# Expert results kept as rows in DRAM by indirect DMA, and the loop over expert passes written out

## The reference, cut to what matters

```python
top_v, top_i = lax.top_k(logits, TOP_K)          # 2 of 8 experts per token
gates = jax.nn.softmax(top_v, axis=-1)
comb = jnp.sum(jax.nn.one_hot(top_i, N_EXPERTS) * gates[..., None], axis=1)
for e in range(N_EXPERTS):
    y = y + comb[:, e:e + 1] * ((silu(h @ we_gate[e]) * (h @ we_up[e])) @ we_down[e])
x = x + y                                        # then a final RMSNorm
```

## Time and profile before

| | |
|---|---|
| median of 3 runs | 1300.16 us (1299.64 to 1300.19) |
| the profiled execution's own time | 1300.49 us |
| its span in the profile | 1298.7 us |
| PE busy | 1247.0 us, 96% |
| DVE busy | 1033.6 us, 80% |
| ACT busy | 828.6 us, 64% |
| POOL busy | 70.6 us, 5% |
| DMA | 351.69 MB, mean 271 GB/s |
| expert passes in the span | about 502 to 1286 us |

### The profile page before, as it was taken

The page is one execution under the profiler, slowest core; times in us unless marked ns, Lnnn a source line. Parts: engine busy times, 40 slices in busy tenths (PEclk is TensorE's granted clock), DMA queues, the critical chain, the costliest instruction groups (busy, mean ns, idle before and its releaser), DMA issues.

```text
span 1298.7 us, 18756 instructions
## 1 busy us (share of the span) xinstructions
PE 1247.0 (96%) x6921; PEld 1063.0 (82%) x6921; DVE 1033.6 (80%) x963; ACT 828.6 (64%) x751; POOL 70.6 (5%) x75
## 2 busy tenths in 40 slices
PE   6988999999999988999999999999999999999996
PEld 5977899999898777888888888888888888888885
DVE  5889564444478957889989989989989989989986
ACT  5656554444455644677677677677777677677674
POOL 3220000000012000000000000000000000000000
PEclk9999999999999998999999999999999999999999
DMA  9940465566436044999999999999999999999970
GB/s 273 337 130 17 146 195 188 172 191 191 134 113 213 17 152 158 348 381 355 343 383 350 347 380 350 344 382 348 346 382 350 345 381 348 348 380 353 340 288 32
DMA packets 180166, 351.69 MB, mean 271 GB/s; under 512 B 8678, under 2 KB 68380, under 8 KB 180124
## 3 DMA queue, kind: packets, MB, share of 16 engines
q1 hardware_dynamic: 178108, 343.77, 75.7%
q0 software_dynamic: 2016, 7.34, 1.6%
HBM read 348.99 MB, written 2.10 MB: 270 GB/s over the span
## 4 chain that ended last, share of the span: by engine, by line
PE 81%; DVE 11%; ACT 2%; issue 2%; SPq 1%; DMA 1%; DVEq 0%; ACTq 0%
PE YB L1619 20%; PE WBS L1606 13%; PE WBS L1607 12%; PE WBS L1608 12%; PE YB L1324 5%; DVE acc L848 4%; PE WBS L1264 3%; PE WBS L1266 3%; PE WBS L1265 3%; DVE w_lo L787 2%; PE YB L1307 2%; PE YB L1634 1%; DVE att L890 1%; DMA raw<-in_w_in 1%; ACT w_hi L488 1%
## 5 line engine op out<-in xcount | busy, mean ns | idle before, releaser
L787 DVE TENSOR_TENSOR w_lo<-raw,w_hi 128x2048 fp32r<-128x2048 f32 x325 | 739.1, 2289 | 124.6 <-ACT w_hi L488 121.1
L488 ACT ACTIVATE w_hi<-raw 128x2048 fp32r<-128x2048 f32 x325 | 617.4, 1916 | 147.6 <-PE YB L1619 67.2
L1606 PE MATMUL WBS<-w_hi,t_hi 128*128 128x512 f32 (+1 forms) x768 | 290.5, 378 | 1.4 <-DVE t_lo L1194 1.4
L1607 PE MATMUL WBS<-w_lo,t_hi 128*128 128x512 f32 (+1 forms) x768 | 285.8, 372 | 0.0
L1608 PE MATMUL WBS<-w_hi,t_lo 128*128 128x512 f32 (+1 forms) x768 | 285.7, 372 | 0.0
L1606 PEld LDWEIGHTS WBS<-w_hi,t_hi 128*128 128x128 f32 x768 | 144.6, 188 | 26.2 <-issue 1.5
L1608 PEld LDWEIGHTS WBS<-w_hi,t_lo 128*128 128x128 f32 x768 | 144.4, 188 | 26.2
L1607 PEld LDWEIGHTS WBS<-w_lo,t_hi 128*128 128x128 f32 x768 | 144.6, 188 | 24.3
L1264 PE MATMUL WBS<-t_hi,w_lo 128*128 128x256 f32 x448 | 127.4, 284 | 0.0
L1265 PE MATMUL WBS<-t_hi,w_hi 128*128 128x256 f32 x448 | 126.7, 283 | 0.0
L1266 PE MATMUL WBS<-t_lo,w_hi 128*128 128x256 f32 x448 | 126.7, 283 | 0.0
(11 more groups left out here) (262 smaller groups left out, 1425.6 us busy)
## 6 DMA issues: line engine op xcount, KB each, us to landing
raw<-in_we_gate SPq DMA_DIRECT2D x88, 1024.0 KB, 5.4
raw<-in_we_up SPq DMA_DIRECT2D x88, 1024.0 KB, 5.6
raw<-in_we_down SPq DMA_DIRECT2D x88, 1024.0 KB, 5.9
raw<-in_w_in SPq DMA_DIRECT2D x20, 1024.0 KB, 5.7
raw<-in_wd_gate SPq DMA_DIRECT2D x11, 1024.0 KB, 5.3
raw<-in_wd_up SPq DMA_DIRECT2D x11, 1024.0 KB, 5.4
raw<-in_wd_down SPq DMA_DIRECT2D x11, 1024.0 KB, 5.0
raw<-in_w_out SPq DMA_DIRECT2D x8, 1024.0 KB, 10.9
```

What stands on the lines that cost most here:

```text
L488: act.activation(w_hi[:, hi_slot(n), :], raw[slot][:], ACT.Copy).then_inc(hi_ready, 1)
L787: dve.tensor_tensor(w_lo[slot][:], raw[slot][:], w_hi[:, hi_slot(n), :].bitcast(F32), ALU.subtract).then_inc(lo_ready, 1)
L1606: pe.matmul(bank, xs_hi[:, k0 + k, :], hi[:, k, :], start=start, stop=False)
L1607: pe.matmul(bank, xs_hi[:, k0 + k, :], lo[:, k, :], start=False, stop=False)
```

## The change

The results of the first seven experts are no longer scattered by PE. A DRAM tensor `y_rows` of 1 + 2 x 256 rows gets row 1 + t for the first choice of token t, 257 + t for its second, and row 0 for slots without a token. POOL fills it with zeros from `att` in layer 1. DVE works out the rows (`dest_of`), and a third column of `mark` carries them through `pick`. At u = 2 ACT writes the result times the gate into `h`, POOL stores it by an indirect DMA (`store_rows`), and `selT`, the low part, the scatters and their adds are gone for these seven; nor are zeros scattered in the first pass. In the eighth pass POOL loads the rows back (`load_rows`), and DVE adds them to `X` at u = 16 and u = 30 (`sum_rows`). The eighth expert's result still goes through PE at the end. The loops over passes are written out for the eight experts; a loop for further items stands behind an `If`, which isn't taken here.

```diff
         h_stored, rows_ready_at, xg_ready, xg_turned = sem("h_stored"), sem("rows_ready_at"), sem("xg_ready"), sem("xg_turned")
         rows_taken = sem("rows_taken")
 
         h_rows = nc.dram_tensor("h_rows", [T, D], F32, kind="Internal").ap()
+
+
+        y_rows = nc.dram_tensor("y_rows", [1 + 2 * T, D], F32, kind="Internal").ap()
+        STORED = NE - 1
+        SUM_AT = [16, 30]
+        zeros_stored, y_stored, y_loaded, y_summed, dest_ready = (sem(s) for s in (
+            "zeros_stored", "y_stored", "y_loaded", "y_summed", "dest_ready"))
 
         block = ctx.enter_context(nc.Block())
...
@@ -438,6 +448,10 @@
                     pool.wait_ge(added, 2 * TT)
                 pool.memset(cu[:, :, 0:PAD], 0.0).then_inc(pads_ready, 1)
                 pool.memset(att[:], 0.0).then_inc(pads_ready, 1)
+                if l:
+                    pool.wait_ge(pads_ready, 2 * L)
+                    for k in range(2 * TT):
+                        pool.dma_start(y_rows[1 + P * k:1 + P * (k + 1), :], att[:].rearrange("p r a i -> p (r a i)")).then_inc(zeros_stored, 16)
 
                 for n in range(len(LEVELS) - 1):
                     pool.wait_ge(decay_ready, 8 * l + n + 1)
...
@@ -464,13 +478,40 @@
             for t in range(TT):
                 pool.wait_ge(normed, 3 * TT + t + 1)
                 pool.dma_start(h_rows[P * t:P * (t + 1), :], h[:, t, :]).then_inc(h_stored, 16)
+            pool.wait_ge(zeros_stored, 16 * 2 * TT)
             pool.wait_ge(h_stored, 16 * TT)
             pool.wait_ge(meta_ready, 1)
-            n_items = pool.value_load(meta[0:1, 0:1], min_val=NE, max_val=ITEMS)
-            with pool.Fori(0, n_items) as i:
+            def fetch_rows(i):
+
                 pool.wait_ge(rows_ready_at, i + 1)
                 pool.sem_inc(rows_taken, 1)
                 pool.indirect_dma_start(xg[:], None, h_rows[:, :], bass.IndirectOffsetOnAxis(rows_at[:, 0:1], 0)).then_inc(xg_ready, 16)
+
+            def store_rows(i):
+
+                pool.wait_ge(y_hi_ready, i + 1)
+                pool.wait_ge(dest_ready, i + 1)
+                pool.indirect_dma_start(y_rows[:, :], bass.IndirectOffsetOnAxis(dest_at[:, i % 2:i % 2 + 1], 0), h[:, i % 2, :], None).then_inc(y_stored, 16)
+
+            def load_rows(t):
+
+                for rank in range(2):
+                    r0 = 1 + T * rank + P * t
+                    pool.dma_start(h[:, rank, :], y_rows[r0:r0 + P, :]).then_inc(y_loaded, 16)
+
+            for i in range(NE):
+                if i:
+                    store_rows(i - 1)
+                if i == STORED:
+                    pool.wait_ge(y_stored, 16 * STORED)
+                    load_rows(0)
+                fetch_rows(i)
+            pool.wait_ge(y_summed, 2)
+            load_rows(1)
+            last = pool.value_load(meta[0:1, 0:1], min_val=NE - 1, max_val=ITEMS - 1)
+            with pool.If(last > NE - 1):
+                with pool.Fori(NE - 1, last) as k:
+                    fetch_rows(k + 1)
 
 
         @block.scalar
...
@@ -540,6 +581,8 @@
                 def coarse(n):
 
                     act.wait_ge(level_done, 9 * l + n + 1)
+                    if l and n == 1:
+                        act.wait_ge(zeros_stored, 16 * 2 * TT)
                     s = LEVELS[n]
                     for r in range(2):
                         bank = YB[:, 2 * (n % 2) + r, :]
...
+
                 preload(ACT.Silu)
                 for u in range(N_FF):
                     if u >= 2:
                         hi(MOE0 + u, i)
-                    if u == 2:
+                    if u == 2 and prev is not None:
 
                         act.wait_ge(unit_used, i * N_FF + MOE0)
-                        y_part()
+                        if stored:
+                            if prev >= 2:
+                                act.wait_ge(y_stored, 16 * (prev - 1))
+                            act.activation(h[:, prev % 2, :], YB[:, 0:2, :].rearrange("p a c -> p (a c)"), ACT.Copy,
+                                           scale=slot_gate[:]).then_inc(y_hi_ready, 1)
+                        else:
+                            y_part()
                     for c in range(EC):
                         if TURN[c] + 2 == u:
                             act.wait_ge(eT_done, i * EC + (c + 1))
...
@@ -1100,6 +1158,8 @@
 
             dve.tensor_tensor(lead[:, :, 0], top[:, :, 1], top[:, :, 0], ALU.subtract).then_inc(lead_ready, 1)
             dve.tensor_tensor(chosen, first, second, ALU.add).then_inc(choice_ready, 1)
+            step(dve.tensor_scalar(score, second, float(T), 1.0, ALU.mult, ALU.add))
+            step(dve.tensor_tensor(dest_of[:].rearrange("p e t -> p t e"), score, each(mark[:, :, 0:1]), ALU.add))
             dve.wait_ge(lead_exp, 1)
             step(dve.tensor_scalar(lead[:, :, 2], lead[:, :, 1], 1.0, None, ALU.add))
             step(dve.reciprocal(lead[:, :, 3], lead[:, :, 2]))
...
-                dve.tensor_copy(picked[:], bank[:, 0:2]).then_inc(picked_ready, 1)
-
-            def turn_rows(count):
-
-                dve.wait_ge(picked_ready, count)
-                dve.tensor_scalar(selT[:], token_row[:], picked[:, 0:1], None, ALU.is_equal)
+                dve.tensor_copy(picked[:], bank[:, 0:3]).then_inc(picked_ready, 1)
+
+            def turn_rows(i, stored):
+
+                dve.wait_ge(picked_ready, i + 1)
+                if stored:
+                    if i:
+                        dve.wait_ge(y_hi_ready, i)
+                    if i >= 2:
+                        dve.wait_ge(y_stored, 16 * (i - 1))
+                    dve.tensor_copy(dest_at[:, i % 2:i % 2 + 1], picked[:, 2:3]).then_inc(dest_ready, 1)
+                else:
+                    dve.wait_ge(y_hi_ready, i)
+                    dve.tensor_scalar(selT[:], token_row[:], picked[:, 0:1], None, ALU.is_equal)
                 dve.tensor_copy(slot_gate[:], picked[:, 1:2]).then_inc(selT_ready, 1)
 
 
             for t in range(TT):
                 ins = dve.tensor_scalar(sel[:, t, :], slot_no[:], place[:, t, 0:1], None, ALU.is_equal)
             ins.then_inc(sel_ready, 1)
+            dve.tensor_copy(mark[:, :, 2], dest_of[:, 0, :])
             dve.tensor_copy(mark[:, :, 1], comb[:, :, 0]).then_inc(cur_ready, 1)
 
             step(dve.tensor_copy(slot_of[:, 0:NE, :].rearrange("p e t -> p t e"), place))
...
-            dve.wait_ge(y_zeroed, 1)
-            with dve.Fori(0, n_items) as i:
+            def sum_rows(t):
+
+                dve.wait_ge(y_loaded, 16 * 2 * (t + 1))
+                for rank in range(2):
+                    ins = dve.tensor_tensor(X[:, t, :], X[:, t, :], h[:, rank, :], ALU.add)
+                    ins.then_inc(y_summed, 1)
+                    dve.wait_ge(y_summed, 2 * t + rank + 1)
+                if t:
+                    dve.memset(started[:, 0:1], 0.0).then_inc(y_lo_ready, STORED)
+                    dve.memset(started[:, 1:2], 0.0).then_inc(scattered, 4 * STORED)
+                    dve.memset(started[:, 2:3], 0.0).then_inc(quad_added, 4 * STORED)
+
+            def expert(i, prev, stored=True):
+
                 for u in range(N_FF):
                     if u >= 2:
                         lo(MOE0 + u, i)
-                    if u == 2:
-                        y_part(i + 1)
+                    if u == 2 and not stored:
+                        y_part(i)
+                    if stored and i == STORED and u in SUM_AT:
+                        sum_rows(SUM_AT.index(u))
                     for r in range(4):
-                        if SCATTER[r] + 2 == u:
-                            add_quad(r, i * 4 + (r + 1), YB[:, 2, :])
+                        if not stored and SCATTER[r] + 2 == u:
+                            add_quad(r, prev * 4 + (r + 1), YB[:, 2, :])
                     for c in range(EC):
                         if TURN[c] + 2 == u:
                             dve.wait_ge(eT_hi_ready, i * EC + (c + 1))
...
                 for u, (what, c, part) in enumerate(plan):
@@ -1619,13 +1708,13 @@
                                     ins = pe.matmul(YB[:, half, :], a[:, f, :], w[:, k, HALF * half:HALF * (half + 1)],
                                                     start=(first and s), stop=(last and e))
                     ins.then_inc(unit_used, 1)
-                    if u in SCATTER:
+                    if u in SCATTER and not stored:
                         r = SCATTER.index(u)
                         if r == 0:
-                            pe.wait_ge(y_hi_ready, i + 1)
-                            pe.wait_ge(y_lo_ready, i + 1)
+                            pe.wait_ge(y_hi_ready, i)
+                            pe.wait_ge(y_lo_ready, i)
                         else:
-                            pe.wait_ge(quad_added, i * 4 + (r + 1))
+                            pe.wait_ge(quad_added, prev * 4 + (r + 1))
                         scatter(r, YB[:, 2, :])
                     if u in TURN:
                         tc = TURN.index(u)
...
```

(32 more changed lines are left out.)

73 lines of the change are left out of this document (39 added, 34 removed).

## The result

The changed kernel takes **1277.55 us** (median of 4 runs, 1277.48 to 1277.74), beside 1300.01 (median of 4, 1299.64 to 1300.19) for the one before: a ratio of 0.9828, interval 0.9811 to 0.9845. That is 22.5 us faster. The kernels of the experiments were timed on several chips, each beside the kernel before, whose medians there were 1300.09 to 1300.52; the ratios go by these, and microseconds of different experiments can be compared to within some 0.5.

A forecast was written before the change was run, and what follows sets the result against it. PE, full in the expert passes, was taken as the bound. The profiled 1300.49 us, less 15.7 for scatters, plus 2.7 for sums, gave 1287.5; the median, 0.33 lower, 1287.2 us; range 1284.0 to 1293.5.

The forecast's parts named there:

- The scatters: PE in the passes: dropping four scatters a pass saves 1.96 us each, 15.7 us over eight passes.
- the 0.04 over two matmuls: PE units with a scatter: slower pitch behind it; if due to the place, the gain is 14.7, not 15.7.
- DVE and ACT keep up at 2.72: Units 2 to 6 without scatters: DVE and ACT allow 2.72 us a unit, since they lose work too.
- Rival 2: DVE and ACT need 3.22 us a unit anyway, PE waits for w_lo; 1295 to 1303 us; chance 0.05.
- The sums: DVE adds in the last pass at u = 16 and 30 delay PE: 2.7 us together, between 1 and 5.3.
- Rival 4: Sums of the last pass late or dearer, loads back waiting for slow stores: 1290 to 1293 us; chance 0.08.
- Costed at nothing: Zeros, stores, loads back, DVE's router steps and loop boundary taken as free; end jump taken as 0, up to 2 us.
- the jump at the end: Each engine jumps over the unused loop after the passes: 0, up to 2 us if it loads code.
- Rival 1: Transfers become the bound at 357 GB/s, a pass needing 99.9 us: 1304 us; chance 0.06, a third reaching 1304.
- Rival 3: Written-out passes make PE load 28 more code blocks: gain gone at 0.45 us each, 1310 at 0.8; chance 0.03.
- The boundary of the loop: Between passes PE shows no gap in six of them, so writing out the loop gives nothing.
- a chain behind PE's own turns, which the change leaves alone: PE's short gaps before down units, 30 in six passes, 10.4 us in all, were expected to stay.

The follow-up runs named there:

- tiles_160: Kernel before with the unused tile idle 160 bytes larger, so later tiles stand where the changed kernel has them; 1292.95 us, ratio 0.9939.
- out_and_160: Kernel before with idle 160 bytes larger and its passes written out on all engines, scatters kept; 1290.02 us, ratio 0.9919.
- the six distances tried here: Start of eT less that of the weight parts, modulo 256 bytes, moved by resizing tiles; changed kernel 1277.55 us at 0, 1283.44 at -32.

## Why the prediction was right and where it was wrong

The 22.5 us are three things: **7.1** from the placement (1300.01 to 1292.95), **2.9** from writing out (to 1290.02), **12.5** from the exchange of scatters for stores. The prediction had the third, at 13.0 (15.7 less 2.7), and had nothing for the other two. Ends of the last unit in the four traces say much the same: 1286.2, 1278.5, 1275.4, 1263.2 us, so 7.7, 3.2 and 12.2.

These steps hold some time that need not be the code's. From the end of the mixer's last unit to the end of the passes' first the four traces take 26.9, 27.3, 26.7 and 26.3 us, at a granted clock of 0.64 to 0.67 up to the passes' first matmul, and the tail behind the last unit is 13.1 in `tiles_160` where it is 12.5 in the other three. What stands outside these two stretches (the passes, where PE ran at the full clock, and the 1.5 us before them) gives **8.0** for the placement (1.5 before the passes, 6.5 in them), **2.5** for writing out and **11.7** for the exchange, and 0.7 is left for the stretch between.

- **The scatters: right as a difference, a little too dear as a price.** u = 3 to 6 fell to 2.72, 2.72, 2.72 and 3.20, 1.95 a pass for a forecast of 1.96. But 0.14 of it was the placement of `selT`, and four scatters cost 1.81 where the tiles lie well. I had seen the 0.04 over two matmuls and had asked whether it "belongs to the place and not to the scatter", meaning the place in the order of the work. It belonged to the place in memory. The lower end, 14.7, was the better value of this term: measured 8 x 1.82 = 14.6.
- **DVE and ACT keep up at 2.72: right.** Rival 2 fell; PE shows no wait for `w_lo` from 595 to 1170 us.
- **The sums: right,** 2.77 for 2.7, in size and in place: 1.57 at unit 17 (forecast 1.5), 0.95 at unit 30 and 0.27 at unit 32 (forecast 1.2 for the two). Rival 4, dearer sums, fell too.
- **Costed at nothing, and so it was:** the stores, issued seven times from 599.0 to 1168.8 us and landed after 7.0 us in the median; the loads back, which landed in time for DVE at 1209.83 without an idle time ahead of it; the zeros, with which the last unit before the passes ends at 477.24, as it does in `out_and_160`, which has none; the jump at the end, which stands in PE's and DVE's idle time behind the last unit, 12.5 us before and after. PE waits there as it did:

```profile
1265.82 0.47 PE L1667 MATMUL WBS<-t_hi,selT 128*128 128x512 f32 x1 [2.62 <-DVE t_lo L1236]
```

- **Rival 1, the transfers, fell.** 377 GB/s at a share of 1.03 in the passes, and 393 with four times the stores, for 200 us on end. The row that had spoken against it, 400 GB/s over 8 us, was the right one; the share of 1.00 in the earlier trace rows was no limit.
- **Rival 3, code loading, fell.** The queue of code (q8) carries 57 packets, 0.93 MB, over the whole span, where it was 29; these are the 28 more that the rival had counted. They cost nothing: from 700 to 1100 us PE is busy 399.96 of 400.
- **Wrong: "The boundary of the loop: PE shows no gap in six of them, since the stretch of rows 2 is full, so writing it out gives nothing."** The boundary does cost nothing: over it the first matmul follows the last by 0.23 us, the usual pitch. But a loop's price isn't only at its boundary. It was in PE's short gaps before down units, which I took for "a chain behind PE's own turns, which the change leaves alone". At u = 8 half of the 0.5 us between the last matmul of unit 7 and the first of the down unit was PE's register steps and separate waits. The range's lower end allowed for "the shorter waits of constants helping PE's gaps a little"; measured it is 0.22 a pass for PE, 0.31 with all engines, 2.5 us over the eight passes and 2.9 by the medians.
- **Missing: a term for where the tiles lie.** "I take 15.7, since the rest of the unit is the same code" treats the same code as the same time, and the sum carries over all that lies outside the scatters unchanged, the down units at 2.81 us among it. Two new tiles and a longer one, 160 bytes in all, took 7 to 8 us off work that the change doesn't mention; a down unit then took 2.72. It could have been asked beforehand: 12 matmuls of one shape took 2.72 us in gate and up units and 2.81 in down units (the first timeline above), with nothing waited for in either. This is the main cause of the miss: 1277.55 and 7.1 are 1284.6, just inside the range. With both terms away the exchange alone would have given 1300.01 - 12.5 = 1287.5, beside the forecast of 1287.2.

The Trainium skill ("Runtime: NRT & Kernel Launch", "Instruction fetch mechanics") advises to unroll, because of stalls for fetching at taken branches. Unrolling did pay here. But what it saved stands at u = 8, behind a wait, and not at the branch back, so no run here shows that reason. The prediction said that by this rule the loop before would lose time at every pass; but the queues of code move nothing between 620 and 1200 us in the kernel before, so nothing was fetched at the branch back and the rule's case didn't arise.

## What to carry to other kernels

A change that adds or resizes any tile moves all later ones, and that alone can be worth more than the change; before a difference is put down to the code, run the old kernel with dead bytes in the place of the new tiles, and compare the pitch of matmuls that nobody touched. Where PE is full, try stationary and streamed tiles that start at the same place modulo 256 bytes, the best of the six distances tried here. Look for the price of a loop in the short gaps after a wait, where register steps can't run ahead, and put additions of a full engine in small pieces where it has slack: eight halves cost nothing where four wholes cost 2.77 us.

## What the runs showed of the hardware

- A 128x512 matmul on split parts has a pitch of 0.227 us (2.72 / 12) at distance 0, 0.229 at -64, and 0.233 to 0.234 at -32, 32, 96 and 128, at the full granted clock in all. It is seen in the down units and the dense channel mixer, and at 0, 96 and 128 in the scatters, and follows the distance and not the absolute place.
- The 16 DMA engines carry 393 GB/s over 200 us, one core running. The share of busy time read 1.00 at 358 and 1.04 at 393, so a share of 1.00 doesn't say that no more goes through. A limit wasn't reached.
- With transfers that dense the time from issue to landing grows, 7.0 to 10.5 us for 1 MB between 377 and 393 GB/s, while nothing waited for it.
- Waits on constants instead of register values took some 0.24 us off one restart of PE a pass (unit 8: 3.17 to 2.93 at the old placement, 3.11 to 2.87 with the 160 bytes), behind a wait for a late `w_lo`. Apart from unit 32, which gains where the other engines' loops go, no other unit showed it.
- The same code behind the last unit took 12.5 us in the kernel before and 13.1 in `tiles_160`, with a granted clock of 1.00 and 0.74 over its first 4.5 us.
